# A gated mixture of experts on one core: turning the hidden rows on VectorE, and the order of the two branches

## The reference, cut to what matters

```python
logits = xt @ w_router; top_v, top_e = lax.top_k(logits, 2); gates = softmax(top_v)
# every token goes to 2 of 8 experts; each expert computes for its tokens
y_e = (silu(x @ w1[e]) * (x @ w3[e])) @ w2[e]      # 1024 -> 3584 -> 1024
y[token] += gate * y_e                              # then layernorm(ALPHA*x + y + e)
```

## Time and profile before

| | |
|---|---|
| median of three runs | 2682.72 us (2681.34 to 2685.76) |
| the profiled execution's own time | 2682.92 us |
| its span, first to last instruction | 2681.1 us |
| granted TensorE clock, mean | 0.997 |
| TensorE busy | 2587.8 us (97%) |
| experts (first `e13` matmul to last scatter) | 793.85 to 1722.3 us of the span |

### The profile page before, as it was taken

The page is one execution under the profiler, slowest core; times in us unless marked ns, Lnnn a source line. Parts: engine busy times, 40 slices in busy tenths (PEclk is TensorE's granted clock), DMA queues, the critical chain, the costliest instruction groups (busy, mean ns, idle before and its releaser), DMA issues.

```text
span 2681.1 us, 66962 instructions
## 1 busy us (share of the span) xinstructions
PE 2587.8 (97%) x30946; PEld 2040.6 (76%) x30946; DVE 1241.0 (46%) x1650; ACT 969.5 (36%) x1339; POOL 181.7 (7%) x185
## 2 busy tenths in 40 slices
PE   8999999999989999999999999999899999989999
PEld 7977899897776666666666666588779978877997
DVE  6677655657750000000000001377567867756685
ACT  4555433355530000000000000256446645654563
POOL 1001000000000000000000000101600000160000
PEclk9999999999999999999999999999999999999999
DMA  6345755454459999999999999752134445313443
GB/s 219 136 160 191 291 180 181 137 199 164 151 192 396 393 391 413 388 412 392 398 404 390 412 387 416 289 171 104 50 119 174 165 173 187 111 50 112 164 177 108
DMA packets 99851, 639.98 MB, mean 239 GB/s; under 512 B 11664, under 2 KB 17296, under 8 KB 29808
## 3 DMA queue, kind: packets, MB, share of 16 engines
q1 hardware_dynamic: 85392, 598.61, 58.5%
q0 software_dynamic: 8352, 34.28, 4.3%
q10 hardware_dynamic: 5824, 2.75, 0.3%
HBM read 630.75 MB, written 13.24 MB: 240 GB/s over the span
## 4 chain that ended last, share of the span: by engine, by line
PE 80%; DVE 11%; ACT 4%; issue 3%; DMA 1%; SPq 0%; DVEq 0%; ACTq 0%
PE ps L1008 32%; PE ps L734 13%; PE ps L736 13%; PE ps L735 13%; DVE wlo L1919 3%; ACT whi L1450 1%; DMA raw<-in_units_dram 1%; PE ps L1308 1%; PE ps L1132 1%; ACT s L1802 1%; PE ps L1287 1%; PE ps L1319 1%; DVE s L2278 0%; DVE mx L2240 0%; PE ps L942 0%
## 5 line engine op out<-in xcount | busy, mean ns | idle before, releaser
L1919 DVE TENSOR_TENSOR wlo<-raw,whi 128x2048 fp32r<-128x2048 f32 (+5 forms) x250 | 531.5, 2134 | 307.6 <-ACT whi L1450 307.0
L1008 PE MATMUL ps<-raw,xe 128*32 128x256 f32 x10752 | 593.2, 379 | 3.6 <-DVE xe L2031 2.6
L1008 PEld LDWEIGHTS ps<-raw,xe 128*32 128x32 f32 x10752 | 359.7, 110 | 221.9 <-issue 11.5
L1450 ACT ACTIVATE whi<-raw 128x2048 fp32r<-128x2048 f32 (+4 forms) x252 | 447.8, 1780 | 204.4 <-PE ps L736 188.1
L736 PE MATMUL ps<-xTh,wlo 128*128 128x256 f32 x1480 | 418.2, 283 | 0.0
L2461 DVE TENSOR_TENSOR hb<-ps,hb 128x384 f32<-128x384 f32 x56 | 31.2, 557 | 834.4 <-ACT hb L1628 834.4
L735 PE MATMUL ps<-xTl,whi 128*128 128x256 f32 x1480 | 417.4, 282 | 0.0
L734 PE MATMUL ps<-xTh,whi 128*128 128x256 f32 x1480 | 417.1, 282 | 0.0
L1008 PE MATMUL ps<-raw,hTe 128*32 128x256 f32 x5376 | 293.4, 379 | 0.0
L734 PEld LDWEIGHTS ps<-xTh,whi 128*128 128x128 f32 x1480 | 280.2, 189 | 0.8 <-issue 0.7
L735 PEld LDWEIGHTS ps<-xTl,whi 128*128 128x128 f32 x1480 | 278.5, 188 | 0.1
(11 more groups left out here) (585 smaller groups left out, 3293.8 us busy)
## 6 DMA issues: line engine op xcount, KB each, us to landing
raw<-in_units_dram SPq DMA_DIRECT2D x544, 1024.0 KB
raw<-in_units_dram SPq DMA_DIRECT2D x18, 512.0 KB
raw<-in_units_dram SPq DMA_DIRECT2D x6, 768.0 KB
raw<-in_units_dram SPq DMA_DIRECT2D x8, 544.0 KB
raw<-in_units_dram SPq DMA_DIRECT2D x6, 688.0 KB
g<-in_b_gate_dram POOLq DMA_DIRECT2D x16, 256.0 KB, 8.0
raw<-in_units_dram SPq DMA_DIRECT2D x4, 576.0 KB
rows_y<-yb ACTq DMA_DIRECT2D x14, 144.0 KB, 5.7
```

The source lines that it names most:

```text
L1008: ins = self.e.matmul(bands(ps[r:r + 32, 256 * i:256 * i + 256]), G.x[:, kk, o:o + 32], w[:, k, :, c:c + 128], start=(kk == 0 and i != 1), ...
L1450: self.e.activation(self.m.hi[u % NHL][:, 0:n], self.m.raw[u % NRAW][:, 0:n], ACT.Copy) \
L1919: self.e.tensor_tensor(self.m.lo[u % NHL][:, 0:n], self.m.raw[u % NRAW][:, 0:n], self.m.hi[u % NHL][:, 0:n].bitcast(F32), ALU.subtract) \
```

## The change

Five edits, all of them inside or at the edges of the expert block.

1. **Transposition.** In the common case the "across" of TensorE and ScalarE is gone. After its product VectorE transposes `hb` in blocks of 32x32 straight into `hTe` (one instruction per column block, 128x384). A block transposition stays inside 32 partitions, so each strip must hold 128 features of its own: in `e13`, strip `b` now holds features 128`b` and round `i` the tokens 32`i` and on. The rows of `w2` are put in the matching order on the host. `Tensor.fill` still gives out a PSUM tile for "across", which nobody writes.
2. **Branches.** The condition is turned round: the common case comes first and falls through, the general case lies behind it, and the engine jumps over it at the end. GpSimd now branches too and reads the count register.
3. **Fewer rows.** In the common case the gather for experts 1 to 7 is one transfer of 96 rows (it was two of 128), "lift" transposes 96 rows, and `xe` is copied 96 wide.
4. **Stores.** `rows_y` is stored in the order in which `yb` lies: two transfers of 768 and 256 columns (four with pieces of 128 columns before); "combine" undoes the order with two VectorE operations in place of one.
5. **Order and filler.** In expert 0's lift VectorE copies `xe` before `gated(2)`; `awake` before ("n0", 0) issues eight products, not six.

```diff
-        with self.e.If(self.most > SLOTS):
+        with self.e.If(self.most <= SLOTS):
+            self.tiles = 1
...
+        with self.e.Else():
             self.tiles = 2
...
-        self.awake(ps, {("n0", 0): 6, ("f20", 1): 3, ("f21", 1): 3}.get((tag, t), 0))
+        self.awake(ps, {("n0", 0): 8, ("f20", 1): 3, ("f21", 1): 3}.get((tag, t), 0))
...
                 r, c, o = 32 * b, 128 * (i if b < 3 else 3), 32 * (b if b < 3 else i)
+                if g[0] == "e13":
+                    c, o = 128 * b, 32 * i
...
         if not pair and j % 2 == 0:
-            e.wait_ge(*self.at("hTe", ex, j // 2))
+            e.wait_ge(*self.at("hTd" if self.tiles == 1 else "hTe", ex, j // 2))
...
+        n = SLOTS if self.tiles == 1 else 128
         for c in range(2):
             for k in range(4 * c, 4 * c + 4):
-                ins = e.transpose(ps[:, k * 128:k * 128 + 128], m.xg[:, 0, k * 128:k * 128 + 128], m.ident[:, :])
+                ins = e.transpose(ps[:, k * 128:k * 128 + n], m.xg[0:n, 0, k * 128:k * 128 + 128], m.ident[0:n, 0:n])
...
-        ps = self.fill(("ac", ex, cb), ("hTe", ex, cb))
+        ps = self.fill(("ac", ex, cb), ("hTd" if self.tiles == 1 else "hTe", ex, cb))
+        if self.tiles == 1:
+            return
         e.wait_ge(*self.at("ev", "e13", ex, cb))
-        if self.tiles == 1:
-            for k in range(3):
-                ins = e.transpose(ps[:, k * 128:k * 128 + 128], m.hb[:, cb % 2, 0, k * 128:k * 128 + 128], m.ident[:, :])
...
-            if self.tiles == 1:
-                ps = bands(self.psum("ac", ex, cb), 8)[:, 0:3, :]
-                e.activation(m.hTe[:, 4 * cb:4 * cb + 3, 0:96], ps[:, :, 0:96], ACT.Copy)
-                ins = e.activation(m.hTe[:, 4 * cb + 3, 0:96].rearrange("p (i n) -> p i n", i=3), ps[:, :, 96:128], ACT.Copy)
...
+        turned = ("hTd",) if self.tiles == 1 else ("full", "ac")
         if cb > 1:
-            e.wait_ge(*self.at("full", "ac", ex, cb - 2))
+            e.wait_ge(*self.at(*turned, ex, cb - 2))
...
+                    e.dma_start(rows[0:96, 0:768], m.yb[0:96, 0, 0:768]).then_inc(*self.c.up("stored", by=16))
+                    e.dma_start(rows[0:96, 768:1024].rearrange("(i p) n -> p i n", p=32),
+                                m.yb[96:128, 0, 0:768].rearrange("p (i n) -> p i n", i=3)) \
...
         elif what == "lift":
+            e.wait_ge(*self.at("full", "xe", a[0], 1))
+            n = SLOTS if self.tiles == 1 else 128
+            e.tensor_copy(m.xe[:, 4:8, 0:n], bands(self.psum("xe", a[0]), 8)[:, 4:8, 0:n]) \
+                .then_inc(*self.up("d_moe", ("xe", a[0], 1)))
             if a[0] == 0:
                 self.gated(2)
...
                 e.tensor_tensor(hh, ps[:, 0:768].rearrange("p (i c n) -> p i c n", i=3, c=2)[:, :, 1, :], hh, ALU.mult) \
                     .then_inc(*self.up("d_moe", ("ev",) + g))
+                e.wait_ge(*self.prev)
+                e.transpose(m.hTe[:, 4 * cb:4 * cb + 4, 0:96].rearrange("p s (i n) -> p i s n", i=3),
+                            m.hb[:, cb % 2, 0, 0:384].rearrange("p (i s n) -> p i s n", i=3, s=4)) \
+                    .then_inc(*self.up("d_turn", ("hTd", ex, cb)))
                 return
...
+            if ex and self.tiles == 1:
+                self.taken("xg0", ("xg", ex, 0), m.xg[0:SLOTS, 0, :], w["xd"], m.idx[0:SLOTS, 0:1])
+                return
```

More of the change, by code:

```diff
@@ L50, in __gt__, with __le__ @@
     def __gt__(self, other):
+        return self
+    def __le__(self, other):
         return self
@@ L579, in experts @@
         n = dict(self.c.n)
-        with self.e.If(self.most > SLOTS):
+        with self.e.If(self.most <= SLOTS):
+            self.tiles = 1
+            for j in range(j0, j1):
+                self.step(j)
+        few, self.prev = self.prev, None
+        least = {k: v for k, v in self.c.n.items()}
+        self.restore(state)
+        self.c.n = n
+        with self.e.Else():
             self.tiles = 2
@@ L583, in experts @@
                 self.step(j)
[L584 to L589, removed]
+        self.prev = few
+        self.c.n.update(least)
     def state(self):
@@ L1127, in across @@
         e, m = self.e, self.m
-        ps = self.fill(("ac", ex, cb), ("hTe", ex, cb))
+        ps = self.fill(("ac", ex, cb), ("hTd" if self.tiles == 1 else "hTe", ex, cb))
+        if self.tiles == 1:
+            return
         e.wait_ge(*self.at("ev", "e13", ex, cb))
-        if self.tiles == 1:
-            for k in range(3):
-                ins = e.transpose(ps[:, k * 128:k * 128 + 128], m.hb[:, cb % 2, 0, k * 128:k * 128 + 128], m.ident[:, :])
[L1133 to L1138, removed]
+        for k in range(4):
+            for t in range(2):
+                o = k * 256 + t * 128
+                ins = e.transpose(ps[:, o:o + 128], m.hb[:, cb % 2, t, k * 128:k * 128 + 128], m.ident[:, :])
+        ins.then_inc(*self.c.up("mm_low", ("full", "ac", ex, cb)))
     def scatter(self, q):
@@ L2020, in do @@
             if ex:
-                for h in range(2):
+                for h in range(2 if ex == 1 else self.tiles):
                     e.wait_ge(*self.at("xg", ex - 1, h))
@@ L2553, in combine @@
             e.wait_ge(*self.prev)
-            e.scalar_tensor_tensor(y, m.yg[:, s, :], m.gz[:, s, t:t + 1], y, ALU.mult, ALU.add) \
-                .then_inc(*self.up("d_moe", ("combined", t)))
+            rows = m.yg[:, s, :].rearrange("p (i c n) -> p c i n", i=4, c=2)
+            for c in range(2):
+                y = m.y1[:, t, 512 * c:512 * c + 512].rearrange("p (i n) -> p i n", i=4)
+                ins = e.scalar_tensor_tensor(y, rows[:, c], m.gz[:, s, t:t + 1], y, ALU.mult, ALU.add)
+            ins.then_inc(*self.up("d_moe", ("combined", t)))
     def route(self):
@@ L2861, in __init__, with state, restore, experts @@
         self.landed = []
+    def state(self):
+        return super().state(), len(self.landed)
+    def restore(self, state):
+        super().restore(state[0])
+        del self.landed[state[1]:]
+    def experts(self, j0, j1):
+        self.e.wait_ge(*self.at("cnt"))
+        self.most = self.e.value_load(self.m.cnt[0:1, 0:1], min_val=0, max_val=256)
+        super().experts(j0, j1)
     def load(self, key, dst, src):
@@ L2883, in run @@
         self.load(("cmask",), m.cmask[:, :], a["c_cmask"])
-        for step in self.p.order:
-            self.do(step)
+        super().run()
     def do(self, step):
@@ L2954, in do @@
             e.wait_ge(*self.at("full", "e13", 7, 0))
-            for h in range(2):
+            for h in range(self.tiles):
                 e.wait_ge(*self.at("xg", 7, h))
```

49 lines of the change are left out of this document (24 added, 25 removed).

## The result

The changed kernel takes 2648.5 us (median of four runs, 2648.0 to 2650.0); the kernel before, timed beside it, 2683.8 us. The ratio is 0.9866 with a 95% interval of 0.9852 to 0.9879. The forecast was 2651.5 us in a range of 2645 to 2662. The two profiled executions have spans of 2681.1 and 2648.2 us: 32.9 us, where the sum had 31.4. The medians differ by 35.3 us; the profiles account for 32.9 of them.

What follows compares the result with a forecast made beforehand. TensorE was taken to bound the kernel, with transfers following closely. Gains of 25.1 (experts 0 to 6), 2.2 (expert 7), 4.1 (start) and 0 (end) sum to 31.4 us off 2682.9: 2651.5 us, range 2645 to 2662.

Steps and rivals of the forecast that it cites:

- Across numbers 0 to 4 and 6: TensorE transpositions in each expert: five at 0.62 us, number 1 at 0.48; 3.58 us an expert, 25.1 for experts 0 to 6.
- Number 5: Across at the expert's end, before e2: a wait for the second PSUM tile takes its place; gain 0, not 0.7 us.
- The period: TensorE's time from one expert to the next: 114.6 us before, 111.0 us after.
- The transfers' price: Weights, gather and stores of one expert: 108.8 us of transfers, some 2 us below TensorE's 111.0.
- I keep experts 0 to 6 whole: Experts 0 to 6 keep their full 25.1 us gain, as TensorE still leads and five buffers cover the unevenness.
- the transfers become the bound: Rival in the experts: weights at 400 GB/s, 112.2 us an expert, 2661.5 us; sign, raw waits in middle experts; chance 0.18.
- Expert 7: Last expert, with extra traffic: 4.3 us offered, 1.6 to 2.5 turn into wait for weights; gain 2.2 us.
- The transposition's cost: VectorE's 128x384 transposition per column block: about 0.56 us, and possibly much longer unseen.
- The start: Start of the expert block: no stall at the condition and xe copied before gated(2); gain 4.1 us.
- The end: End of the expert block: jumps, longer filler and clock together net 0, between -1.7 and +3 us.
- TensorE's jump: Behind the last scatter: priced at 2.54 us, so the filler ends 1.2 us after the rmsnorm's result.
- the rival: Jumps cost more than they free: start stall stays, or half-speed filler delays transposes 3 us; 2654 to 2657 us, chance 0.13.

Runs made afterwards that it cites:

- e13: Not a run, no time of its own: code name of each expert's products before VectorE's product, which follows ScalarE's silu.
- kernel with idle transposes: Changed kernel plus three identity transposes on TensorE, read by nobody, at each of the 56 old across places: 2676.8 us, ratio 0.9968.
- e2: Not a run, no time of its own: code name of each expert's products behind the lift, which read the transposed hTe.
- kernel with half of the products: Changed kernel without the second row block's products of each expert weight unit, all transfers kept: one run, experts 867.98 us, 108.7 us between lifts on average.
- two kernels without the tile wait: Changed kernel not waiting for e2's unwritten second PSUM tile: 2645.1 us, 0.9845; the same with one 512 KB load moved from expert 7 to 3: 2643.9 us, 0.9848.
- kernel with six: Changed kernel with six filler products ahead of the rmsnorm's transposes, as before, in place of eight: 2647.5 us, ratio 0.9867.

## Why the prediction was right, step by step

- **The total agrees better than its parts.** The stretches that the change touches gained 30.6 us for 31.4: the experts 1.9 less than forecast, start and end 0.4 and 0.7 more. The 2.3 us of the stretches that the change doesn't touch, which bring the profiles' difference to 32.9, are luck: nothing in the prediction stands for them.
- **Across numbers 0 to 4 and 6: right.** The kernel with idle transposes puts 22.6 to 24.0 of the 25.4 us back.
- **Number 5, a wait in its place: right.** 0.50 us in front of `e2` in seven experts, gone when the wait is, with `e2` 1.31 us behind the last `e13` product, where it was 986.25 - 984.89 = 1.36 before. The lift's 0.65 was right for its old neighbour and 0.15 short for its new one, which the wait absorbs.
- **The period: right.** 110.97 us without transfers in the way, 111.0 forecast. The terms were less exact than the sum: the restarts were worth 0.9 us an expert, not 0.7 (in the kernel before the piece behind "index" took 10.77 us, not 10.50), and "index", which now stands directly behind products, took 0.2 of it back (0.54 for 0.34).
- **The transfers' price: right**, 108.7 for 108.8 us an expert. What failed is the step from there to "I keep experts 0 to 6 whole": a margin of 2 us on average doesn't empty a ring of five buffers of its bad moments. Six periods lost 2.0 us in one profile of the changed kernel and 3.5 in the other. The rival "the transfers become the bound" (400 GB/s) didn't happen; its marker was met, its size was not. The prediction called 407 GB/s the slowest stretch of its kind, and that was a misreading: the stretch from 1160 to 1221 us, out of which it took the gather's share, ran at 400 GB/s. By its own sum, 44.8 MB at 400 are 112.0 us, above TensorE's 111.0. Neither figure was a limit: in the kernel before the transfers followed TensorE, at 399 GB/s on average from 900 to 1500 us, and a full share of the DMA engines is read there as at 414. Only the kernel with half of the products shows what they can do, 414. Here the prediction's conclusion held although one of its two supports didn't.
- **Expert 7: right.** 4.2 us of wait for 2.3, so 1.9 more, where 1.6 to 2.5 were forecast.
- **The transposition's cost: right**, 0.58 us, unseen.
- **The start: 4.5 us for 4.1.** Branch and order can be told apart: 1.6 by the order, and 2.9 are left for the branch, whose gap was 2.54, and for the copy of `xe`, now 96 wide (0.56 us for 0.68); with a clock that falls in the gap the branch is worth 4.0. The gather was in time here; in the two kernels without the tile wait it wasn't, and their lifts waited 0.75 and 0.69 us for it and their starts are 0.6 to 0.7 us longer.
- **The end: 0.7 us for 0.** The mis-sized term is TensorE's jump: 0.31 us in this profile, not 2.54. So the filler ended 0.83 us ahead of the rmsnorm's result, not 1.2 behind it, and the clock stayed up, worth 0.7 and, by the kernel with six, up to 1.85. Why this jump is short, and 2.65 us in the kernel with half of the products, isn't shown. That 9 us of scatter products stand ahead of it doesn't explain it alone, since the same 8.96 us stood ahead of both. So the forecast's price for this jump was met in one kernel of eleven, and there the transposes came late as the rival had it; the prediction didn't foresee that the changed kernel would be spared. (The Trainium skill, Runtime: NRT & Kernel Launch, Instruction fetch mechanics, says that a taken branch out of the fetched pages must fetch its target first. The runs agree that the stall goes with the jump: no kernel has the gap where it has no jump. The page gives no size.) ScalarE's jump was 2.27 us against my 2.54 and was covered, as said, by GpSimd's 9.01 us: VectorE's additions ended 12.84 us behind the scatter's start, 12.83 in the kernel before.
- **Edits 3 and 4**: the prediction gave the gather and the stores 2.1 us less transfer time an expert and no gain of their own; no gain is what the runs show. The narrower lift and copies of edit 3 were not run by themselves.

## What to carry to other kernels

When a step is taken off a busy engine, look for what else its time was covering: of the seven transposes here one gave nothing, because its 0.48 us had been hiding a wait, for a tile that the common case never writes. Price the resource that follows closely (here the weight stream) by an average, but expect waits before the average is reached, since a shallow ring of buffers has to survive the worst few microseconds. And put the common case where it falls through, with the jump at a point where another engine's work covers it; leave room for a jump of up to 2.7 us, since its size wasn't the same in every kernel here.

## What the runs showed of the hardware

- A gap of 2.54 us left TensorE's clock at full speed in the kernel before, a gap of 2.74 us at the same place was followed by 2.9 us at half speed (granted clock 0.53 in 787 to 790 us), and gaps of 2.93 and 3.08 us by 6 and 3.4 us of it. So a stall of some 2.6 us cost itself alone, or half as much again.
- The same kind of far jump cost TensorE 2.54 and 2.74 us in front of a weight unit. Behind the scatter it cost 0 to 1.00 us in ten kernels and 2.65 us in one. On ScalarE it showed as 1.2 to 2.7 us in nine kernels and not at all in two.
- VectorE's transposition of 128x384 in blocks took 0.578 us, 1.5 ns an element column, about as much as a product of two operands of that shape (0.56 us).
- Eight transposes of 96 rows took 0.66 us directly behind a transpose and 0.81 behind products in strips; four products of "index" 0.34 and 0.54.
- Weights, stores and gathers together ran at 414 GB/s over 540 us when nothing else held them back, and the products of the experts ran at the same 54 ns each whether the transfers moved 406 or 208 GB/s beside them.
